# Filled projection products issued as two 64-column halves of the stationary

## The reference, cut to what matters

```python
proj = jnp.einsum('bld,dp->blp', h, prm['w_in'][l])          # 2048 -> projected columns
r = zs[..., :RWKV_WIDTH]
k = zs[..., RWKV_WIDTH:2 * RWKV_WIDTH]
v = zs[..., 2 * RWKV_WIDTH:o]
...
def step(S, inp):
    rt, wt, kt, vt, at, bt = inp
    sa = jnp.einsum('bhij,bhj->bhi', S, at)
    S = S * wt[:, :, None, :] + sa[..., None] * bt[:, :, None, :] + vt[..., None] * kt[:, :, None, :]
    return S, jnp.einsum('bhij,bhj->bhi', S, rt)
```

## Time and profile before

| | before |
|---|---|
| median of 3 runs | 2006.02 us (2004.7 to 2013.86) |
| profiled execution: time, span | 2006.03 us, 2004.5 us |
| mean granted clock | 0.961 |
| PE busy | 1825.5 us (91%), 10397 matmul records |
| records of line 698 | 672, mean 457 ns, 223.2 us busy |
| DVE, ACT, POOL busy | 526.5, 316.1, 335.1 us |
| data moved | 573.86 MB, mean 286 GB/s |

### The profile page before, as it was taken

How to read it: one execution, slowest core, us unless ns; L and a number is a source line. 1 busy time by engine, 2 the same in 40 slices (tenths; PEclk the granted TensorE clock), 3 DMA queues, 4 the chain that set the end, 5 groups by cost and what they waited for, 6 DMA issues and landing times. The chain is left out here.

```text
span 2004.5 us, 26562 instructions
## 1 busy us (share of the span) xinstructions
PE 1825.5 (91%) x10397; PEld 970.8 (48%) x10397; DVE 526.5 (26%) x1232; ACT 316.1 (16%) x674; POOL 335.1 (17%) x489
## 2 busy tenths in 40 slices
PE   4579999999999996799969999999999999999996
PEld 2137665555555564577534334353443535344342
DVE  2142244454345445101231120111112021111203
ACT  2001122122222212100311101011110101111002
POOL 0020012122112211200000040311304022130403
PEclk9669999999999999899889999999999999999998
DMA  9894357455545726455219999999999999999992
GB/s 304 302 334 109 93 155 228 145 187 176 153 175 162 230 96 174 136 159 188 84 49 429 428 427 428 428 429 428 422 429 429 429 429 429 429 427 429 428 428 107
DMA packets 191107, 573.86 MB, mean 286 GB/s; under 512 B 10691, under 2 KB 114461, under 8 KB 165363
## 3 DMA queue, kind: packets, MB, share of 16 engines
q1 hardware_dynamic: 187230, 563.76, 72.9%
q0 software_dynamic: 3200, 6.20, 1.3%
q10 hardware_dynamic: 631, 3.27, 0.6%
HBM read 567.78 MB, written 5.65 MB: 286 GB/s over the span
## 5 line engine op out<-in xcount | busy, mean ns | idle before, releaser
L1766 PE MATMUL PS<-ring,xt 128*64 128x512 f32 x2048 | 492.5, 603 | 26.7 <-DMA ring<-in_w_up 25.2
L1766 PEld LDWEIGHTS PS<-ring,xt 128*64 128x64 f32 x2048 | 194.7, 138 | 290.5 <-issue 246.9
L1973 POOL TENSOR_TENSOR x<-x,tmp 128x512 f32<-128x512 f32 (+1 forms) x96 | 125.2, 1308 | 668.9 <-DVE tmp L1890 668.9
L1799 PE MATMUL PS<-ring,att 128*64 128x512 f32 x1024 | 227.5, 593 | 0.0
L698 PE MATMUL PS<-ring 128*128 128x320 f32 x672 | 223.2, 457 | 0.0
L1799 PEld LDWEIGHTS PS<-ring,att 128*64 128x64 f32 x1024 | 116.8, 137 | 95.6 <-issue 58.3
L1890 DVE TENSOR_TENSOR tmp<-PS,catT 128x512 f32<-128x512 f32 (+1 forms) x96 | 66.1, 689 | 299.8 <-PE PS L1753 296.2
L364 PE MATMUL PS<-ring,silT 128*32 128x512 f32 x768 | 109.2, 694 | 39.0 <-DMA ring<-in_w_ada 36.8
L698 PEld LDWEIGHTS PS<-ring 128*128 128x128 f32 x672 | 116.5, 191 | 49.3 <-issue 12.9
L1418 PE MATMUL PS<-catT,ring 128*128 128x320 f32 x512 | 138.5, 432 | 0.0
L1901 DVE TENSOR_TENSOR sgt<-sgt,PS 64x1024 f32<-64x1024 f32 x16 | 19.4, 1213 | 424.8 <-ACT sgt L1829 424.8
(11 more groups left out here) (411 smaller groups left out, 1652.8 us busy)
## 6 DMA issues: line engine op xcount, KB each, us to landing
ring<-in_w_gate SPq DMA_DIRECT2D x64, 2048.0 KB, 12.5
ring<-in_w_up SPq DMA_DIRECT2D x64, 2048.0 KB, 16.3
ring<-in_w_down SPq DMA_DIRECT2D x64, 2048.0 KB, 15.8
ring<-in_w_ada SPq DMA_DIRECT2D x48, 2048.0 KB, 9.0
ring<-in_w_in SPq DMA_DIRECT2D x34, 1024.0 KB, 5.9
ring<-in_w_out SPq DMA_DIRECT2D x16, 1024.0 KB, 6.0
x_a<-in_x_prompt ACTq DMA_DIRECT2D x2, 1024.0 KB, 8.0
sraw<-in_state_wkv POOLq DMA_DIRECT2D x8, 256.0 KB, 3.7
```

Source lines behind the costliest of these rows:

```text
L1766: m = nc.tensor.matmul(PS[C * g:C * g + C, c, :], xt[:, 4 * q + k, :], unit(2 * q + g, FE)[:, k, 512 * c:512 * c + 512], start=(q == 0 and ...
L1799: m = nc.tensor.matmul(PS[C * (c % 2):C * (c % 2) + C, 4 + c // 2, :], att[:, 2 * q + k, :], unit(u, D)[:, k, 512 * c:512 * c + 512], star ...
L1973: nc.gpsimd.tensor_tensor(xx, xx, tmp[0:n_, r % 2, :], ALU.add).then_inc(x_ok, 1)
```

## The change

Each filled product is issued as two, one for each half of the 128 columns of the stationary, with its result on the matching half of the partitions. Both read the same moving operand. The semaphore is raised by the second half of the last step. The products of the first pair, ahead of the pair loop, stay whole. `half` is the pair of slices 0 to 63 and 64 to 127.

```diff
                 if k == 0:
                     pe.wait_ge(ld_w[j], WBASE[j] + 16 * (i + 2))
                     pe.wait_ge(z_done, i + 1)
-                m = nc.tensor.matmul(PS[:, j, 0:T], wbuf[:, j, k, :], hT[:, k, :], start=(k == 0), stop=(k == KT - 1))
+                for r in half:
+                    m = nc.tensor.matmul(PS[r, j, 0:T], wbuf[:, j, k, r], hT[:, k, :], start=(k == 0),
+                                         stop=(k == KT - 1), skip_group_check=True)
                 if k == KT - 1:
                     m.then_inc(wu[j], 1)
```

## The result

The changed kernel takes 1992.5 us (median of 20 runs, 1985.4 to 2005.5) beside 2007.4 us for the kernel before (20 runs, 2000.0 to 2017.2). The ratio is 0.9929, 95% interval 0.9912 to 0.9945: 14 us faster by the ratio and 15 by the medians, where 20 were forecast. The profiled execution took 1990.4 us, with a span of 1988.8 us and a mean granted clock of 0.955 (before: 2004.5 us and 0.961).

A forecast was written before the change was run, and what follows sets the result against it. PE was taken to set the pace, busy 66.03 of a pair's 69.85 us. 0.43 + 3.16 - 0.70 = 2.89 us a pair, seven pairs 20.2, less 0.25: 2006.0 - 20.0 = 1986.0 us, range 1979 to 1996.

The forecast's parts named there:

- rival 2: In the scan, DVE's and ACT's answers take most of the gain: 10.5 us in all, 1995 us; chance 0.12.
- The price of a product in halves: Each filled product: two halves side by side cost 0.54 us, the same as whole; taken from L1766 in the expert stage.
- The switches: A lone product between 64-column groups pays 0.15 + 0.20 = 0.35 us for going to 128 columns and back.
- The ten in the scan: F_G but the first, F_U and F_ST: 3.16 us gained a pair, bounds 2.2 and 3.5; a chunk from 3.24 to 2.28.
- F_MM and the first F_LEVEL: Between 64-column groups, from L808 to L819: 0.43 us gained a pair, bounds 0 and 0.54.
- The later F_LEVEL: Other five F_LEVEL and the transposes: DVE's and ACT's answers decide, gain 0; L819 to L819 stays at 16.87 us.
- the cover of F_TOK: PE's waits at L780, L792 and L799 (0.5, 1.7, 0.6 us) hide F_TOK's switches: cost 0, otherwise 0.35 us.
- The loss at the end of the pair: F_END and the last eight products, among 128-column groups: two round trips, 0.70 us lost a pair, bounds 0.5 and 0.8.
- the halves don't run side by side: Each of the 336 products: halves wait for each other wholly or partly, up to about 2167 us; chance 0.06.
- the switches at the end: Rival: end-of-pair switches cheaper or hidden, scan chunk at PE's own 2.19 us; 25 us gained, 1981 us; chance 0.12.
- An excess that belongs to any long record after short ones: Rival: first 320-column record after short ones costs the 0.35 us in either form; time stays 2006 us; chance 0.05.
- I carry a shift of their start to the end one to one: Mixing and expert stages after the pairs keep their length, so the pairs' 20.0 us gain reaches the end whole.

The follow-up runs named there:

- all-halves kernel: The changed kernel, every filled product in the pair loop issued as two halves, against the kernel before: median 1992.9 us over three sets, ratio 0.9929.
- the F_TOK: Halves only in F_TOK, three products of a pair, all others whole, against the kernel before: 2007.9 us, ratio 0.9993.
- F_PREP kernel: Halves only in F_PREP, eleven products of a pair, all others whole, against the kernel before: 2005.8 us, ratio 0.9982.
- the spare products: Two, three or five extra whole products once in the first pair, all products in halves: 1993.2, 1996.8, 1993.9 us against 1992.7 without.

## Why the prediction was right, and where it was off

**The time** fell into the stated range of 1979 to 1996, but not by the forecast's own account. A gain of 14.9 us in the medians is outside the 16 to 24 that it gave itself; the range reached so far only for rival 2, whose mechanism did not come about. In the number, that is luck. The pair stage is another matter: its sum came true term by term.

**The price of a product in halves** was right: 0.54 us, by 32 records in 4.46 with a switch in them, and its condition, halves side by side, was shown by taking it away. The row that it was taken from is less near than the prediction says: the two products of L1766 share one stationary of 64 columns and have different moving operands, while here the stationary differs and the moving operand is shared. A round of L1766 took 0.433 us for 512 columns and one here 0.269 for 320, which is the same for each column within 1%.

**The switches** were right in place and size: 0.35 us for a round trip from 64 columns to 128 and back. The ten in the scan were forecast to give 3.16 us against the floor of the answers and gave 3.20; the chunk was forecast at 2.28 and took 2.27. F_MM and the first F_LEVEL gave 0.47 (5.63 to 5.16; 0.43 forecast). The later F_LEVEL gave nothing: L821 to L821, the groups of the earlier trace rows, take 16.86 us (490.32 to 507.18), as forecast, with a new wait of PE on DVE in each round:

```profile
PE PS L794 <- DVE bk L1159: 1.7, 1, 1.7
PE PS L821 <- DVE inv L1178: 1.4, 5, 0.3
PE PS L782 <- DVE rk L1149: 0.6, 1, 0.6
PE PS L810 <- ACT ring L1016: 0.5, 1, 0.5
PE PS L801 <- DVE bv L1173: 0.4, 1, 0.4
```

These are PE's waits from 462.90 to 529.79. Against the earlier trace rows, L801's wait has shrunk from 0.6 to 0.4: the cover of F_TOK has paid for its switches. The loss at the end of the pair was forecast at 0.70 and was 0.69: L910 to L917 takes 6.95 us where L908 to L915 took 6.36, and 0.10 more lie behind L917. The answers that were expected to make L887 wait don't show as a wait in this list; they show as 0.59 from L699 to L887 (515.81 to 516.40) where the next group without an answer follows in 0.55 or less.

**The rivals.** That the halves don't run side by side is excluded: 16 rounds and a switch took 4.46 us, 0.16 above 16 x 0.269, which is the switch, so no weight load of a round shows. The Trainium skill ("TensorE: Matmul & The Clock Gate", The mechanism) says that a weight load overlaps matmuls in flight only where its row group differs, and also that a load for the background weight buffer is pulled ahead of them. These loads share all rows, took 138 ns each and were hidden, so the first of the two rules does not hold here. It spoke no more against the halves than against the whole products, whose loads share all rows as well and are hidden too, at 0.269 us a record. The answers did not take most of the gain: the scan gave 3.20 us where 3.16 were forecast. Nor were the switches at the end cheaper: they cost 0.69 us where 0.70 were forecast. An excess that belongs to any long record after short ones is excluded too: it is gone between groups of the same form.

**The step that failed** is "I carry a shift of their start to the end one to one". The pairs gave 19.8 of the 20.0 us, the medians 14.9. Most of what lies between goes with time at half clock. Over all 32 runs of the all-halves kernel it is 176 us (standard error 2), over the 58 of the kernel before 164 (1.5). Among runs of one and the same kernel, a us more at half clock goes with 0.29 us more of time (172 runs, correlation 0.75), so these 12 us are worth 3.4. The mean times, 2008.6 and 1993.9, differ by 14.8 (standard error 1.1), and with those 3.4 the work itself is 18.2 us less, near to the 19.8 of the pairs.

In the two profiled executions the loss does not lie in the pairs: each has two pairs with a stretch at half clock. It lies in the stages up to the first expert, which run at 0.87 instead of 0.90 and take 5.2 us longer with the same instructions, and 1.9 us of it in the experts. How much of this is the change's doing, one trace of each doesn't say. Over the 14 traces those stages take 282.5 to 292.5 us, 0.35 us more for each us at half clock in them (correlation 0.99). The trace of the kernel before is the shortest of all, and the F_TOK and the F_PREP kernel, whose pairs are as long as before, have these windows from the last pair to the first expert:

```profile
753.08:1037.83 284.75, 238.39 (x1308) 158.14 (x1306) 76.27 (x228) 56.11 (x132) 21.29 (x38) 0.89 0.42 130
751.64:1041.40 289.76, 243.43 (x1307) 161.31 (x1305) 76.32 (x228) 56.39 (x132) 21.37 (x38) 0.86 0.41 127
```

The range of the forecast allowed 2 us either way for half clock in the pairs and nothing for the stages behind them.

**What stays open** is why the all-halves kernel spends more time at half clock. F_TOK's and F_PREP's switches don't do it alone. Whether it is the moment at which the later stages begin, the spare products don't tell. One more candidate is in the table and was not followed up: each set of runs with halves in F_END and the last eight has 167 to 184 us at half clock (together 176, standard error 1, 79 runs), and each set without them 157 to 165 (together 163, standard error 1, 93 runs). The kernel with halves there and nowhere else has 173. No trace shows how these halves would act on the stages behind, and no run was made to test it, so this is a pattern and not a cause.

## What to carry to other kernels

A filler matmul should have the column form of the groups that it stands between. Here the form itself was free, each change of form cost 0.15 to 0.20 us, and ten lone fillers a pair were worth 3.2 us, while the same edit among 128-column groups was a loss of 0.7 us; choosing place by place gained 0.63 us more a pair, 4.4 in the kernel (its time fell by more, along with a clock that no run explains). Before counting on it, look for a run of the kernel without fillers: its steps are the floor, and they foretold the new pair to 0.1 us. A gain read from a stage should not be carried to the end without a margin for the granted clock of the stages behind it; here it was worth 3.4 us of 20 between the kernels, and 10 us between single traces.

## What the runs showed of the hardware

Matmuls on different columns of the array overlap beyond the neighbour in program order: with the eight products' halves issued apart, four rounds at the border of the two blocks were shared. A switch from 64 to 128 columns costs more than the way back (0.20 against 0.15 us). And executions of one kernel differ by up to 20 us, along with the time that they spend at half clock, at 0.29 us for each us, so that sets of six runs of the same kernel had means of 0.9538 and 0.9580.
